# A delta-rule layer's rates: columns kept step by step, their products among the tile products, convolutions and transposes moved

## What is computed

```
p = hn @ w_in
qkv, z, b, a, c_q, c_kv, k_pe = split_cols(p, IN_SIZES)
...
q = l2norm(q) * (GDN_DK ** -0.5);  k = l2norm(k)
beta = sigmoid(b)
g = -exp(a_log) * softplus(a + dt_bias)
...
g = jnp.cumsum(g, axis=-1)                       # inside each chunk
decay = where(lower, exp(where(lower, g_i - g_j, 0)), 0)
lmat = where(strict, (k_beta @ k.T) * decay, 0)
amat = lmat + eye(chunk)
sol = triangular_solve(amat, [v_beta, k_beta * exp(g)])
qk = where(lower, (q @ k.T) * decay, 0)
```

## Time and profile before

| | before |
|---|---|
| median of 3 runs | 1018.06 us (1017.28 to 1019.62) |
| the profiled execution | 1017.65 us, its span 1015.8 us |
| PE busy | 974.0 us (96%) |
| DVE, ACT, POOL busy | 513.7, 447.6, 157.8 us |
| chain that ended last | PE 88%, DVE 6%, ACT 3%, issue 2%, DMA 1% |
| tile products of the loop (L598, L599, L600) | 51% of the span in the chain |

### The profile page before, as it was taken

The page is one execution under the profiler, slowest core; times in us unless marked ns, Lnnn a source line. Parts: engine busy times, 40 slices in busy tenths (PEclk is TensorE's granted clock), DMA queues, the critical chain, the costliest instruction groups (busy, mean ns, idle before and its releaser), DMA issues.

```text
span 1015.8 us, 20658 instructions
## 1 busy us (share of the span) xinstructions
PE 974.0 (96%) x8604; PEld 845.0 (83%) x8604; DVE 513.7 (51%) x980; ACT 447.6 (44%) x964; POOL 157.8 (16%) x257
## 2 busy tenths in 40 slices
PE   4999999999989989999999999999999999999997
PEld 4988899877757655666665999999999999999996
DVE  5655766666476387455556543533343344334433
ACT  5545638566635677445446324421332133113212
POOL 1020500245520301344541000000000000000000
PEclk9999969999999999999999999999999999999999
DMA  7312111130023701577772412322222222222202
GB/s 250 117 53 84 43 43 42 42 71 10 2 59 88 248 2 51 182 244 269 242 247 89 155 47 89 100 98 104 84 84 84 84 83 84 87 95 107 87 1 88
DMA packets 31655, 102.58 MB, mean 101 GB/s; under 512 B 14023, under 2 KB 14967, under 8 KB 25218
## 3 DMA queue, kind: packets, MB, share of 16 engines
q1 hardware_dynamic: 22346, 63.50, 19.0%
q0 software_dynamic: 9216, 37.75, 10.8%
HBM read 96.45 MB, written 4.22 MB: 99 GB/s over the span
## 4 chain that ended last, share of the span: by engine, by line
PE 88%; DVE 6%; ACT 3%; issue 2%; DMA 1%; SPq 0%; DVEq 0%; ACTq 0%
PE PS L598 17%; PE PS L600 17%; PE PS L599 17%; PE PS L1082 7%; PE PS L1093 3%; PE PS L1119 3%; PE PS L733 2%; PE PS L1102 1%; PE PS L806 1%; PE PS L837 1%; PE PS L889 1%; PE PS L988 1%; DMA RAW<-in_w_stream 1%; PE PS L580 1%; PE PS L707 1%
## 5 line engine op out<-in xcount | busy, mean ns | idle before, releaser
L598 PE MATMUL PS<-XH,WH 128*128 128x272 f32 (+1 forms) x896 | 261.1, 291 | 0.0
L600 PE MATMUL PS<-XH,WL 128*128 128x272 f32 (+1 forms) x896 | 260.4, 291 | 0.0
L599 PE MATMUL PS<-XL,WH 128*128 128x272 f32 (+1 forms) x896 | 259.5, 290 | 0.0
L1255 ACT ACTIVATE WH<-RAW 128x2048 fp32r<-128x2048 f32 x46 | 88.0, 1913 | 195.9 <-PE PS L600 191.8
L598 PEld LDWEIGHTS PS<-XH,WH 128*128 128x128 f32 x896 | 169.0, 189 | 4.8 <-issue 4.2
L599 PEld LDWEIGHTS PS<-XL,WH 128*128 128x128 f32 x896 | 169.3, 189 | 0.0
L600 PEld LDWEIGHTS PS<-XH,WL 128*128 128x128 f32 x896 | 169.1, 189 | 0.0
L598 PE MATMUL PS<-NH,WH 128*128 128x272 f32 x512 | 149.1, 291 | 0.8 <-DVE WL L1771 0.8
L600 PE MATMUL PS<-NH,WL 128*128 128x272 f32 x512 | 147.6, 288 | 0.0
L599 PE MATMUL PS<-NL,WH 128*128 128x272 f32 x512 | 146.6, 286 | 0.0
L1771 DVE TENSOR_TENSOR WL<-RAW,WH 128x2048 fp32r<-128x2048 f32 (+2 forms) x51 | 108.6, 2129 | 66.6 <-ACT WH L1255 64.8
(11 more groups left out here) (336 smaller groups left out, 1540.7 us busy)
## 6 DMA issues: line engine op xcount, KB each, us to landing
RAW<-in_w_stream SPq DMA_DIRECT2D x47, 1024.0 KB, 4.8
XN<-in_hin SPq DMA_DIRECT2D x4, 512.0 KB, 6.2
out_y_p<-YO SPq DMA_DIRECT2D x4, 512.0 KB, 2.7
CST<-in_big SPq DMA_DIRECT2D x1, 1132.5 KB, 13.1
SS<-in_sstate SPq DMA_DIRECT2D x1, 1024.0 KB, 5.2
out_ssm_s<-SS SPq DMA_DIRECT2D x4, 256.0 KB
CN<-in_cache,IDX POOLq DMA_INDIRECT x64
WQN<-in_wq SPq DMA_DIRECT2D x3, 256.0 KB, 5.8
```

The source lines that it names most:

```text
L598: pe.matmul(PS[:, b, 0:n], wh, xh[:, k, c:c + n], start=(k == 0), stop=False)
L599: pe.matmul(PS[:, b, 0:n], wh, xl[:, k, c:c + n], start=False, stop=False)
L600: last = pe.matmul(PS[:, b, 0:n], wl, xh[:, k, c:c + n], start=False, stop=(k == DT - 1))
L1255: act.activation(WH[w % 2][:, :, :], RAW[w % 2][:, :, :], ACT.Copy).then_inc(sem("w_high"), 1)
```

## The change

The tiles, the matrices and the sums stay as they are. What changes:

BROW is kept by step: column 35 t + u instead of 16 u + t (`by_step`). ACT writes the roots and the sigmoid in that order, DVE scans in the old order and copies the sums over with one instruction more. A column product reads 35 neighbouring columns of each row. The spreads are cut into halves of 280 columns, and DVE reads the banks as (t, u).

On PE the column products, the pair products and the later spreads are given to `weight_tile` as `ready`, which is called ahead of each contraction step:

```diff
+            def among_13(k):
+                if k >= 2:
+                    gate_column(k - 2)
+            def among_14(k):
+                gate_column(6 + k)
+                if k in (1, 6):
+                    spread_half(1, k // 4)
+            def among_15(k):
+                if k < 2:
+                    gate_column(14 + k)
+                if k in (4, 6):
+                    spread_half(2, k // 6)
+                elif k in (1, 2, 3, 5):
+                    gate_pair((1, 2, 3, 5).index(k))
...
-                for t in range(CH):
-                    pe.matmul(PS[:, 5, 0:5 * NU], row("e16", t), BROW[:, :, t:T:CH], start=(t == 0), stop=(t == CH - 1))
+                last = pe.matmul(PS[:, 5, 0:5 * NU], row("e16", t), BROW[:, :, NU * t:NU * t + NU], start=(t == 0), stop=(t == CH - 1))
...
-                    last = weight_tile(i // 2, i % 2, (XH, XL), (b, b + 1), HALVES)
+                    last = weight_tile(i // 2, i % 2, (XH, XL), (b, b + 1), HALVES,
+                                       {13: among_13, 14: among_14, 15: among_15}.get(i))
...
-                    spread_rows(0)
-                elif i == 12:
-                    gates_to_columns()
-                    spread_rows(1)
-                elif i == 13:
-                    spread_rows(2)
-                elif i == 14:
+                    first_spread()
+                elif i == 15:
                     for x in range(4):
                         chunk_transposes(x)
...
                     sum_squares("cq", 3)
+                    gate_products(range(0, 3 * DT))
                     solved_transposes(0)
                     solved_transposes(1)
...
-            gate_products(range(0, 3 * DT + 6))
+            gate_products(range(3 * DT, 3 * DT + 6))
```

```diff
                 elif i == 12:
                     copy_products(2)
+                elif i == 13:
+                    silu_out(10)
+                elif i == 14:
                     rates()
-                elif i == 13:
                     act.wait_ge(sem("dve_step"), DVE_STEP["decay_diff"])
                     act.activation(TMP[:, :, :], TMP[:, :, :], ACT.Exp, scale=-1.0).then_inc(sem("act_step"), 1)
                     last_rates()
-                elif i == 14:
+                    silu_out(11)
+                elif i == 15:
                     act.wait_ge(sem("silu_done"), 12)
                     for x in range(4):
                         copy_chunks(x)
...
             for i, m in enumerate(TILES[:EARLY]):
-                if i % 2 == 0 and i < 16:
+                if i % 2 == 0 and i < 14:
                     weights_low(i // 2 + 1)
-                if m < 12:
+                if m < 12 and i < 12:
                     convolve(CONV.index(m), m)
...
                     by_column(KK, 0)
+                    masked(KK, "m_lower")
+                    link(masked(KQ, "m_updiag"))
+                    convolve(10, TILES[12])
+                    convolve(11, TILES[13])
+                    weights_low(8)
                     rate_products()
-                    link(masked(KK, "m_lower"))
                     decay_differences()
-                    masked(KQ, "m_updiag")
                     link(scaled(KK, 10))
                     link(scaled(KQ, 3))
+                    key_matrix()
+                    by_column(KQ, 2)
+                    query_matrix()
                     rate_exponents()
```

More of the change, by code:

```diff
@@ new lines, in spread_half, with gate_column @@
+            def spread_half(x, half):
+                if x and half == 0:
+                    pe.wait_ge(sem("col_used"), x)
+                    pe.wait_ge(sem("qk_inverted"), 2)
+                c = HALF * half
+                last = pe.matmul(PS[:, 6 + half, 0:HALF], row("hexp"), BROW[:, (3, 1, 4)[x], c:c + HALF], start=True,
+                                 stop=True)
+                if half == 1:
+                    last.then_inc(sem("col_spread"), 1)
+            def gate_column(t):
+                if t == 0:
+                    pe.wait_ge(sem("e16_in"), 16)
+                    pe.wait_ge(sem("dve_step"), DVE_STEP["gates"])
+                    pe.wait_ge(sem("qk_inverted"), 2)
+                    pe.wait_ge(sem("kk_copied"), 2)
+                last = pe.matmul(PS[:, 5, 0:5 * NU], row("e16", t), BROW[:, :, NU * t:NU * t + NU], start=(t == 0), stop=(t == CH - 1))
+                if t == CH - 1:
+                    last.then_inc(sem("pe_step"), 1)
@@ L1890, in by_column @@
                 dve.wait_ge(sem("col_spread"), x + 1)
-                for (c, n), b in zip(HALVES, (6, 7)):
-                    us = slice(c // CH, (c + n) // CH)
-                    last = dve.tensor_tensor(dst[:, us, :], dst[:, us, :], PS[:, b, 0:n].rearrange("p (u t) -> p u t", t=CH),
-                                             ALU.mult)
+                for half in range(2):
+                    part = dst[:, :, CH // 2 * half:CH // 2 * half + CH // 2]
+                    last = dve.tensor_tensor(part, part, PS[:, 6 + half, 0:HALF].rearrange("p (t u) -> p u t", u=NU), ALU.mult)
                 last.then_inc(sem("col_used"), 1)
```

80 lines of the change are left out of this document (37 added, 43 removed).

## The result

The changed kernel takes **1020.1 us** (median of 20 runs, 1017.22 to 1021.74) beside 1018.46 for the kernel before in the same series. The ratio is **1.0015, 95% interval 1.0009 to 1.0022**: slightly slower, where 1011.7 and "faster" were forecast, and outside the range of 1009.4 to 1016.8. The profiled run took 1020.91 us with a span of 1019.1.

A forecast was written before the change was run, and what follows sets the result against it. TensorE's own work near 127 to 152 us, at half clock, was taken as the bound. Up to tile 17, 20.7 us become 13.3; with later waits the gain is 6.4, giving 1011.7 us, range 1009.4 to 1016.8.

The forecast's parts named there:

- (4): Clock over the interleaved tiles 13 to 15: full speed, so the 1.75 us lost at half speed in tile 13 go.
- (5): Wait for the rates ahead of column 0, in tile 13: 1.05 us instead of 1.97, column 0 starting at 126.3.
- (7): End of tile 16: a new PE wait of about 0.65 us for the squares of the ckv norm.
- (8): Serial chain, ACT copies and DVE substitution up to the solved transposes: ends near 185.0, with 0.9 us to spare.
- rival B: The serial chain ahead of the solved transposes binds, 3 us later than forecast: 1013.8 us; chance 0.14.
- (9): Behind the solved transposes: PE waits 1.5 us for TIW; first product on the state at 192.5 instead of 198.97.
- The reading of the stride: Column products of L580: the 16-element stride sets 0.30 us a record at full clock; runs of 35 take 0.163.
- Rival A: Column products: the stride is not what sets 0.30; a column costs 0.73 us, time 1016.2; chance 0.11.
- Its sign: Column records staying 0.30 us apart, instead of the forecast 0.16, would show Rival A.
- (1): Columns among tile products: 0.12 us per interruption (0 to 0.2), 0.45 a column, 7.2 us for 16 against 9.70.
- it stays: Recurrence and all behind it wait for nothing with its own time, so the 6.4 us gain reaches the end.
- Rival C: Clock falls to half again around the columns for 17.1 us, losing 8.5 us: 1020.2 us; chance 0.07.

The follow-up runs named there:

- e2: Changed kernel with its 8-row column products reading columns 16 apart instead of in runs of 35; median 1038.85 us, 1.0191 to 1.0219 of the kernel before.
- e11: Changed kernel with 128 rows in its column products and these reading columns 16 apart; median 1019.14 us, 0.9999 to 1.0018 of the kernel before.
- e4: Changed kernel with column products reading 128 rows of weights and rates, 120 of them zero, instead of 8; median 1015.38 us, 0.9957 to 0.9996 of before.
- e10: Changed kernel with columns (128 rows), pairs and spread 1 in one block behind tile 12; median 1018.06 us, 0.9987 to 1.0007 of the kernel before.
- e13: Kernel before with 8 more tile products, results overwritten, just ahead of the recurrence; median 1021.16 us, 1.0012 to 1.0041 of the kernel before.
- e14: Kernel before with 16 more tile products, results overwritten, just ahead of the recurrence; median 1021.81 us, 1.0023 to 1.0051 of the kernel before.
- e5: Changed kernel with 16 more tile products, results overwritten, just ahead of the recurrence; median 1019.40 us, 1.0004 to 1.0027 of the kernel before.
- e15: e7 with 16 more tile products ahead of the recurrence; median 1011.86 us, 0.9919 to 0.9958 of the kernel before.
- e9: e7 with 12 more tile products in the 2.1 us wait for the masked values; median 1011.42 us, 0.9906 to 0.9947 of the kernel before.
- e8: e7 with the 32 small products of the absorbed queries issued in pairs among key products; median 1017.72 us, 0.9980 to 1.0019 of the kernel before.
- e7: Changed kernel with 128 rows in column products, spreads and pairs; median 1011.07 us, 0.9904 to 0.9938 of the kernel before.

## Why the prediction was wrong, point by point

**Right.** (4) The granted clock was 1.00 from 123.6 to 144.1. (5) Column 0 started at 126.39 for a forecast 126.3, after 0.47 us of wait where 1.05 was forecast, since PE itself came later (it had waited 0.8 us ahead of the last key products); the copies took 1.20, 0.42 and 0.17 us on DVE, more than forecast for the one written by step (0.6 to 0.75) and less for the others:

```profile
124.54 1.20 DVE L1877 COPY BROW<-BROW 8x560 f32<-8x560 f32 x1
```

(7) The new wait ahead of the ckv squares was 0.58 for 0.65. (8) The chain through DVE kept the 0.9 us of room that it was given (it ended at 189.4, the solved transposes began at 190.29, both 4.4 later than forecast), so rival B is out. (9) The wait for TIW was 1.52 for 1.5. The reading of the stride, "something other than the array sets 0.30", was right for full clock: e2 and e11 show it with nothing else changed (0.28 us a column). That agrees with the penalty for each new line that the Trainium skill states ("SBUF — State Buffer", "Door 1: The DMA port swizzle"); at half clock no penalty shows (0.30 against 0.29 us a record), so the 9.70 us of the kernel before, at half clock from 126.98 us on, owed little to the stride. Rival A is out. Its sign, the distance of the two column records, would not have decided: they start 0.26 us apart in the kernel after, between the 0.16 of the forecast and the 0.30 of A.

**Wrong, first: the price of an interruption in (1).** I took 0.12 us and bounded it by 0.2. It is 0.69 - 0.33 = 0.36, because a load of 8 rows is not pulled ahead of the running products and the load behind it isn't either. Sixteen columns then cost 11.0 us, not 7.2. The 3.8 us are as much as the last spread is late (157.23 for 153.4), and most of the 4.5 by which the recurrence is (197.05 for 192.5); the last 0.7 was not traced. Both rows from which I bounded it were misread. The products with TIW among gate products have 128 rows, so they are the free case, as e4 shows. The L555 group is of the dear kind, with its loads of 8 columns, and I counted only the lengthened record behind it, not the gaps ahead of the group and of that record, and with them it comes to nearly 0.3 us (an estimate from the starts of the records). I also read 0.26 us from it as the pace of a record, which has a part of these gaps in it; the columns' own pace is 0.15 (e10), not 0.163. A bound taken from rows of another shape is no bound.

**Wrong, second: "it stays".** I let all that is gained ahead of the recurrence come out at the end, since nothing behind it has a time of its own. I put the clock's part in it at nothing, without a reason. Five microseconds went to half clock near 294 and 335 us, at a wait and at a run of small products that the kernel before has too, without loss. A shift of the kernel by 1 to 3 us brought both of them in the profiled run of e13 and one in that of e14, and took them away in those of e5 and e15. Rival C looked for the clock only in the stretch that is changed; there it didn't fall. That its 1020.2 us stand beside the measured 1020.1 is chance.

**How much of it is chance.** The runs of the kernel after differ among themselves by the clock: three at a mean granted clock of 0.996 took 1017.2 to 1017.5 us, nine at 0.993 a median of 1020.6. Even in the three 0.4% of the span, 4.1 us, is withheld, where it is 0.1% in e5's profiled run, which has no half clock from 105 to 405 us; so they are not the case without dips. An estimate for the change without late dips is its start of 197.05 with the tail of 816.8 of the kernel before, a profiled run 1.9 us faster, and not the 6.4 forecast; with the dips as they come it costs 1.6 in the median. That a late dip can come, and that it comes in some runs of one program and not in others, is shown. What decides it stays open. In e9 and e8 it stood at another place after the edit, by one profile each.

## What to carry to other kernels

- When small products are put among large ones, give their weights the same shape, here 128 rows by 128 columns, with zeros if need be. Here that took a column from 0.69 to 0.32 us and turned 0.15% slower into 0.8% faster (e7), for a few clears on GpSimd beside other work. Look in the weight-load rows for whether the load starts a product ahead. In a block of their own the 8-row products cost no more than those with 128 rows.
- Before a stride or a shape is blamed for a slow block, look at the granted clock over it: at half clock the strided reads cost what reads in runs cost.
- A gain of a few microseconds that moves a long tail is not safe at the end. Add a filler of known length to the kernel before, and see whether the tail's time is the same; if it scatters by more than the gain, judge a change by the start of the tail, and the tail on its own.

## What the runs showed of the hardware

- A read of 175 columns in runs against one with a stride of 64 bytes: 0.28 us more for two float32 records among tile products, with 8 and with 128 rows (e2, e11); in a block 0.30 against 0.15 us a record at full clock and 0.30 against 0.29 at half.
- A weight load of 8 or 64 rows was not pulled ahead of products with 128 rows, and neither was one of 128 rows by 8 columns (L555); with 8 rows this costs 0.37 us for an insertion (e4 against the kernel after).
- The clock can fall to half while PE is busy throughout: strided 8-row products in interleaved form had half clock for 40 us (e2), the same with 128 rows none ahead of the recurrence (e11).
- The same code behind the same wait of 2.09 us ran at full clock in one profiled run (1.98 us, the kernel before) and partly at half in another that came 1.5 us later (2.62 us, e13).
